# A narrower dense tile in a two-branch streaming layer: 192 tokens by gathered expert rows, projected ahead of the other 384

## The reference, cut to what matters

```python
x = x + (g_m * a_m + g_f * a_f + g_c * a_c) @ p['w_out']
x = x + peer_ffn(rmsnorm(x, p['norm_ffn']), wq, keys, u, v)

def peer_block(tok, wq, keys, u, v):
    qr = (tok @ wq).reshape(p, PEER_HEADS, 2, PEER_DQ // 2)
    s = jnp.einsum('phcd,hckd->phck', qr, keys)
    top_s, top_i = lax.top_k(s, PEER_TOPK)
    cand = top_s[:, :, 0, :, None] + top_s[:, :, 1, None, :]
    ids = top_i[:, :, 0, :, None] * N_KEYS + top_i[:, :, 1, None, :]
    best, j = lax.top_k(cand.reshape(p, PEER_HEADS, PEER_TOPK * PEER_TOPK), PEER_TOPK)
    eidx = jnp.take_along_axis(ids.reshape(...), j, axis=-1)
    g = jax.nn.softmax(best, axis=-1)
    act = jax.nn.gelu(jnp.einsum('phkd,pd->phk', u[eidx], tok))
    return jnp.einsum('phk,phkd->pd', g * act, v[eidx])
```

## Time and profile before

| | us |
|---|---|
| median of 3 runs (1950.44 to 1951.83) | 1951.48 |
| the profiled execution | 1951.0 |
| its span in the trace | 1949.3 |
| TensorE busy (97% of the span) | 1888.0 |
| VectorE busy (77%) | 1506.5 |
| GpSimd busy (48%) | 941.9 |
| ScalarE busy (44%) | 859.6 |

### The profile page before, as it was taken

How to read it: one execution, slowest core, us unless ns; L and a number is a source line. 1 busy time by engine, 2 the same in 40 slices (tenths; PEclk the granted TensorE clock), 3 DMA queues, 4 the chain that set the end, 5 groups by cost and what they waited for, 6 DMA issues and landing times.

```text
span 1949.3 us, 34536 instructions
## 1 busy us (share of the span) xinstructions
PE 1888.0 (97%) x12585; PEld 1215.4 (62%) x12596; DVE 1506.5 (77%) x2995; ACT 859.6 (44%) x1313; POOL 941.9 (48%) x586
## 2 busy tenths in 40 slices
PE   9999999999999999999999999998599999999997
PEld 7647777777777776555556666654255555555554
DVE  7975566454355568999899899846798999999885
ACT  6444446555443433333356666642233333333331
POOL 3732222222243353666877777878544445454320
PEclk9999999999999999999999999999799999999998
DMA  5722114223352223777989999999999999999971
GB/s 201 220 100 97 47 55 131 88 86 129 122 155 88 97 77 111 233 271 267 354 281 380 382 378 375 375 326 366 362 379 370 380 394 399 384 400 386 398 284 49
DMA packets 165532, 486.17 MB, mean 249 GB/s; under 512 B 17688, under 2 KB 59744, under 8 KB 164904
## 3 DMA queue, kind: packets, MB, share of 16 engines
q1 hardware_dynamic: 81824, 240.98, 34.4%
q0 software_dynamic: 46208, 167.83, 23.1%
q10 hardware_dynamic: 37384, 75.84, 10.5%
HBM read 419.75 MB, written 64.80 MB: 249 GB/s over the span
## 4 chain that ended last, share of the span: by engine, by line
PE 75%; DVE 14%; POOL 5%; issue 3%; DMA 1%; ACT 1%; ACTq 0%; DVEq 0%; POOLq 0%; SPq 0%
PE ps L2304 27%; PE ps L1847 24%; PE ps L1966 10%; PE ps L1863 3%; POOL w_lo L585 3%; POOL rows L618 3%; DVE rows L1635 2%; PE ps L2120 1%; PE ps L2244 1%; PE ps L2245 1%; DVE eq L1622 1%; DVE eq L1620 1%; PE ps L2100 1%; DVE eq L1619 1%; PE ps L2178 1%
## 5 line engine op out<-in xcount | busy, mean ns | idle before, releaser
L585 POOL TENSOR_TENSOR w_lo<-raw,w_hi 128x1024 bf16<-128x1024 f32 x229 | 503.1, 2201 | 609.6 <-ACT w_hi L695 586.1
L695 ACT ACTIVATE w_hi<-raw 128x1024 bf16<-128x1024 f32 x357 | 374.3, 1051 | 313.8 <-DMA raw<-in_v_units 129.1
L2304 PE MATMUL ps<-W_hi,w_hi 128*128 128x416 bf16 x992 | 337.5, 340 | 25.8 <-DVE W_lo L1771 25.8
L1847 PE MATMUL ps<-act_hi,w_hi 128*128 128x416 bf16 (+1 forms) x1040 | 351.6, 339 | 6.8 <-ACT hb L1055 6.0
L1847 PE MATMUL ps<-act_lo,w_hi 128*128 128x416 bf16 (+1 forms) x1040 | 351.6, 339 | 0.0
L1847 PE MATMUL ps<-act_hi,w_lo 128*128 128x416 bf16 (+1 forms) x1040 | 351.5, 339 | 0.0
L2304 PE MATMUL ps<-W_lo,w_hi 128*128 128x416 bf16 x992 | 337.4, 340 | 0.0
L2304 PE MATMUL ps<-W_hi,w_lo 128*128 128x416 bf16 x992 | 337.4, 340 | 0.0
L618 POOL DMA_INDIRECT rows<-in_v_units,rowi x128 | 170.4, 1331 | 202.1 <-DVE accS L1743 179.8
L1055 ACT ACTIVATE hb<-ps 128x416 f32<-128x416 f32 x128 | 66.2, 517 | 275.9 <-PE ps L1847 261.7
L1721 DVE TENSOR_TENSOR w_lo<-raw,w_hi 128x1024 bf16<-128x1024 f32 x124 | 151.2, 1219 | 43.0 <-ACT w_hi L695 42.9
(11 more groups left out here) (453 smaller groups left out, 3488.4 us busy)
## 6 DMA issues: line engine op xcount, KB each, us to landing
raw<-in_u_units SPq DMA_DIRECT2D x128, 512.0 KB, 5.5
raw<-in_v_units SPq DMA_DIRECT2D x128, 512.0 KB, 10.2
raw<-in_units SPq DMA_DIRECT2D x99, 512.0 KB, 3.3
hd<-hb ACTq DMA_DIRECT2D x128, 224.0 KB, 5.7
Hb<-hd SPq DMA_DIRECT2D x32, 896.0 KB, 8.4
gd<-gsb ACTq DMA_DIRECT2D x48, 448.0 KB, 7.0
Gb<-gd SPq DMA_DIRECT2D x32, 672.0 KB, 6.2
gz<-stage ACTq DMA_DIRECT2D x24, 288.0 KB, 2.1
```

The lines of the kernel that those rows point to most:

```text
L585: pool.tensor_tensor(w_lo[:, k % RING, :], raw[:, k % RAW, :], w_hi[:, k % RING, :], ALU.subtract).then_inc(lo_ready, 1)
L695: act.activation(w_hi[:, k % RING, :], raw[:, k % RAW, :], ACT.Copy).then_inc(hi_ready, 1)
L1847: last = pe.matmul(ps[:, bank + half, 0:n], w[:, slot, col:col + P], x(k)[:, half * n:(half + 1) * n], start=(k == 0 and w is w_hi and x i ...
L2304: ins = pe.matmul(ps[:, d, 0:TDX], w[:, slot, d * P:(d + 1) * P], x[:, k, 0:TDX], start=(first and w is w_hi and x is W_hi), stop=False)
```

## The change

- 192 tokens are gathered: the last 128 as before, and 64 more (`NX` = P/2) that lie two partitions to a token, 64 rows on each. They are now ordinary members of one list of `ND` = 192 dots and 192 sums: `x_dot`, the move across partitions and the separate table are gone. 384 tokens (`TD`) are dense, and everything stored is 384 wide; a block of routes has 48 tokens (`TBLK`), six steps a body, 48 steps in all (`G_BODY`, `N_STEP`).
- Output and query projection run twice, once for the 192 tokens (`NA`) and once for the 384; the 24 units are loaded and split a second time (`U_OUT2`, `U_WQ2`).
- VectorE makes the routes of the first tile between the additions of the second output projection (`out_beside`, `OUT_AT`), and 12 of the dots between the sortings of the second query projection (`DOTS_WQ`, `DOTS_AT`). GpSimd issues 18 fetches in that projection.
- The routing products begin one body sooner (`J_G` 5 for 6), with two dots a step (`DOTS_TWO` = 4, in a pair of steps, for 3); the remaining 44 dots follow, two a unit.
- In the second expert half GpSimd makes the low half of every fourth unit, from unit 7 on (`pool_makes`), VectorE the others. `x_combine` follows every second `combine`.
- SBUF is laid out anew.

```diff
-NX = 32
-TDX = TD - NX
+NX = P // 2
+ND = NST + NX
+T0 = T - NSP
+TD = T0 - NX
+NA = T - TD
...
-J_G = 6
+J_G = 5
...
-G_BODY = 7
+G_BODY = 6
...
+DOTS_WQ, DOTS_AT = 12, 4
...
-DOTS_TWO = 3
+DOTS_TWO = 4
+OUT_AT = (1, 2, 4, 6, 10, 15, 17, 18)
...
+def pool_makes(c):
+
+    return c >= 2 * GRP - 1 and c % GRP == GRP - 1
...
             for c in range(NCH):
                 fetch_v(n_main(c), v_rows, rowi[:, c:c + 1])
-                i = (c - X_COMB) // X_STEP
-                if c == X_COMB + X_STEP * i and 0 <= i < NX:
-                    fetch_v(n_comb(i), v_rows, rowx[:, i:i + 1])
+                if c + GRP < NCH and pool_makes(c + GRP):
+                    pool.wait_ge(hi_ready, U_V + c + GRP + 1)
+                    pool.tensor_tensor(w_lo[:, (U_V + c + GRP) % RING, :], raw[:, (U_V + c + GRP) % RAW, :],
+                                       w_hi[:, (U_V + c + GRP) % RING, :], ALU.subtract).then_inc(v_pool_low, 1)
+                if c % 2:
+                    fetch_v(n_comb(c // 2), v_rows, rowi[:, NST + c // 2:NST + c // 2 + 1])
...
+            for q in range(NHC):
+                dve.wait_ge(s_ready, NHC + q + 1)
+                top16(step1, lambda x: ps[:, 4 + q % 2, x * P:(x + 1) * P], lambda x: rest[:, x, :],
+                      lambda x: top[:, 1 + x, q, :], lambda x: topi[:, 1 + x, q, :], NFT - 1)
+                if 0 <= q - DOTS_AT < DOTS_WQ:
+                    dot(q - DOTS_AT)
...
-            for s in range(NX):
-                x_dot(s)
             dve.wait_ge(b_prod, N_STEP)
             for c in range(NCH + LAG):
                 if c < NCH:
                     gated(c)
-                if N_VLOW <= c + 2 < NCH:
+                if N_VLOW <= c + 2 < NCH and not pool_makes(c + 2):
                     unit_low(c + 2)
...
+            pe.wait_ge(r2_kept, 1)
+            for j in range(KT):
+                n = U_OUT2 + j
+                pe.wait_ge(lo_ready, n + 1)
+                if j == 2:
+                    pe.wait_ge(tk1, 4 * NHC)
+                if j >= 4:
+                    pe.wait_ge(x2_ready, KT + j - 3)
+                tile(n % RING, lambda k: mg_hi[:, k, mB], lambda k: mg_lo[:, k, mB], OUT_BANKS[j % 4], n=TD,
+                     halves=1).then_inc(unit_used, 1)
+                if j == TOK_AT:
+                    turn_tokens()
...
+            pe.wait_ge(x2_ready, 2 * KT)
+            pe.wait_ge(x_kept, 1)
```

More of the change, by code:

```diff
@@ new lines, in _, with turn_tokens @@
+                if q:
+                    key_scores_a(q - 1)
+            key_scores_a(NHC - 1)
+            def turn_tokens():
+                pe.wait_ge(h_scaled, KT)
+                pe.wait_ge(half_kept, NHC)
+                pe.wait_ge(q_evac, NHC)
+                for x in range(KT):
+                    last = pe.transpose(ps[:, 6 + x // 4, x % 4 * P:(x % 4 + 1) * P], hA[:, x, NX:NA], ident[:, :])
+                last.then_inc(tok_turned, 1)
+                for b in range(2):
+                    for x in range(KT):
+                        last = pe.matmul(ps[b * HP:(b + 1) * HP, 2 + x // 4, x % 4 * P:(x % 4 + 1) * P], hA[:, x, 0:NX],
+                                         ident[:, :], start=True, stop=True)
+                last.then_inc(x_turned, 1)
@@ new lines, in key_scores, with token_sums @@
+            def key_scores(q):
+                pe.wait_ge(q_evac, NHC + q + 1)
+                if q >= 2:
+                    pe.wait_ge(tk1, 4 * (NHC + q - 2) + 2)
+                for t in range(NFT - 1):
+                    last = pe.matmul(ps[:, 4 + q % 2, t * P:(t + 1) * P], qrB[:, q % 2, t * P:(t + 1) * P], keys[:, q, :],
+                                     start=True, stop=True)
+                last.then_inc(s_ready, 1)
+            def token_sums():
+                pe.wait_ge(n_add, (KT - 1) * 4)
+                for t in range(NFT - 1):
+                    last = pe.matmul(ps[:, 0, t:t + 1], sqB[:, 0, t * P:(t + 1) * P], ones[:, 0:1], start=True, stop=True)
+                last.then_inc(n_ssq, 1)
@@ new lines, in token_rows @@
+            def token_rows():
+                pe.wait_ge(n_inv, 4)
+                for t in range(NFT - 1):
+                    last = pe.matmul(ps[:, 1, t * P:(t + 1) * P], rB[:, 1, t:t + 1].broadcast_to((P, P)), ident[:, :], start=True,
+                                     stop=True)
+                last.then_inc(r2_spread, 1)
+            pe.wait_ge(x2_ready, 2 * KT)
+            pe.wait_ge(x_kept, 1)
+            for q in range(NHC):
+                n = U_WQ2 + q
+                pe.wait_ge(lo_ready, n + 1)
+                if q >= 2:
+                    pe.wait_ge(q_evac, NHC + q - 1)
+                tile(n % RING, lambda k: xg_hi[:, k, mB], lambda k: xg_lo[:, k, mB], 2 + q % 2, n=TD, halves=1,
+                     ready=None if q else 3 * KT).then_inc(unit_used, 1)
```

645 lines of the change are left out of this document (348 added, 297 removed).

## The result

The changed kernel takes **2085.97 us** (median of 4 runs, 2078.27 to 2095.8) against 1950.96 us for the kernel before on the same chip (4 runs, 1949.81 to 1951.83): ratio **1.0695**, 95% interval 1.0648 to 1.0742. I had predicted 1914 us, in a range of 1872 to 1950, with a chance of 0.12 for slower. The profiled execution took 2078.27 us, with a span of 2076.4 us and a mean granted clock of 0.969.

The account below looks back on a forecast made before the run. DMA was taken to bound the kernel from the routing products on: first routing product at 958 us, second half from 1369, its 512 and 10 us to 1891, tail 21 to 1912, forecast 1914 us; range 1872 to 1950.

Parts of the forecast that it names:

- What bounds it, and what the dense part saves: Whole kernel: DMA as full as TensorE; 384-column tiles save TensorE 82 us over 256 units, 112 us all together.
- The low halves given to GpSimd I cost at nothing, covered by DMA: Second expert half: GpSimd's low halves cost nothing under DMA's 4.18 us a unit; worth 16 us if DMA had room.
- four units' lead: Second expert half: GpSimd's low half stands behind a waiting fetch, but is made four units ahead.
- VectorE's durations in the first half: Stretch of routing products: DMA 300 us and 4 for a slack start, weighed against TensorE; no term for VectorE.
- My slower rival: From 958 us on: DMA falls under 376 GB/s as late units run the queues dry; 1966 us, chance 0.15.
- 103 us: Last 22 units before the second half: DMA moves 41.3 MB at 400 GB/s in 103 us, where TensorE needs 86.
- The part ahead of the experts: Both output and query passes: first expert product at about 773 us in place of 753.8, 19 us given away.
- Hidden, just: Passes of the 192 gathered tokens: GpSimd's 53 us of low halves fit within the 59 us these passes take.
- 396 GB/s: Second half: DMA moves 202.8 MB at 396 GB/s in 512 us, with 10 us more to the last product.
- the two slower rivals: DMA under 376 GB/s, 1966 us, chance 0.15; memory the limit, 346 GB/s at a full share, 2034 us, chance 0.02.
- the 1999 us for a lower bandwidth: The forecast's sum at the Trainium skill's 358 GB/s, one core's share of memory, would end at 1999 us.
- The stall of 25.8 us: TensorE's wait before the second half goes, since all 192 dots are now made in the first half.

Follow-up runs that it names:

- the first experiment: The changed kernel, but VectorE makes all low halves of the second expert half again and GpSimd none: 2049.3 us.
- the run with the least GpSimd work: Changed kernel with 64-column GpSimd low halves from second query pass through first expert half, fetches up to three units earlier, no GpSimd low halves in second half: 1915.85 us.

## Why the prediction was wrong

- **What bounds it, and what the dense part saves: the saving was there.** With GpSimd's subtractions next to gone the kernel ran in 1915.85 us, where I had 1914. The agreement is luck in part: the first routing product came 15 us earlier (943.0 for 958), the routing products were 16 us shorter, and the second half 31 us longer (556.7 for 525.5).
- **"The low halves given to GpSimd I cost at nothing, covered by DMA": the step that failed, in the second half.** They cost 24 us (21 to 25 over the runs). I compared GpSimd's load with the time it had (10.2 of 16 us) and never asked what its 2.20 us do to VectorE's 1.28. Some 14 us came from the order; the other 10 I put down to holding, by the durations. The "four units' lead" was no cover: it made the low half ask for a high half that wasn't there yet, with the next fetch behind it.
- **VectorE's durations in the first half: the step that failed there, and the largest.** I worked the routing stretch out for DMA and TensorE alone, 304 us, and not for VectorE. There 48 steps and 96 dots meet 64 low halves of GpSimd, and each of these costs the stretch 0.7 to 1.0 us (47 to 64 us over 64): with the fetches early VectorE was busy 347.65 of 349.1 us, and with the subtractions short the stretch took 290.9. The kernel before showed it to anyone who compared two groups of one shape. Between 1030 and 1260 us it had:

```profile
L1701 DVE TENSOR_TENSOR hot<-iota,pair 128x1024 bf16<-128x1024 bf16 x41 | 57.3, 1396 | 7.5 <-PE ps L2245 7.5
L1705 DVE TENSOR_TENSOR hot_lo<-hot,pair 128x1024 bf16<-128x1024 bf16 x41 | 28.1, 686 | 0.0
```

  Two operations of the same kind and size, 1396 and 686 ns. One by one, 28 of the 41 took 0.84 us or more, and all 28 lie over a subtraction of GpSimd; the others took at most 0.75. No run took the subtractions out of this kernel, but by what the changed kernel's runs show it was a hold already, paid where VectorE had 16 us of 230 to spare.
- **The fetches' place.** I did not price the order of GpSimd's list in this stretch: each fetch stands behind a low half that waits for ScalarE. That was 17 to 34 us. My slower rival had this chain (a late unit holds a combination, that a fetch, and the queues run dry), with a price of 52 us and a chance of 0.15; its place was the second half, where it proved to be about 14 us.
- **"103 us" for the last 22 units: 134.7.** I had them bound by DMA, and GpSimd bounds them: one low half of 2.2 us and two fetches a unit. With short subtractions the stretch took 110.
- **The part ahead of the experts: 773, measured 787.8.** The pass of the 192 tokens ended at 660.95 us, 14 us late for 647; the 45 us for the second output pass came out. A query unit of the first pass took 2.70 us for my 2.50, some 3 us over the 16, and the rest lies ahead of them, in the output units and the norm. "Hidden, just" weighed GpSimd there against TensorE and not against VectorE. Five of VectorE's eight low halves of the tokens (`xg_lo`, 0.40 us at their shortest) took some 2.0 us, each beside GpSimd's subtractions:

```profile
L1602 DVE SCALAR_TENSOR_TENSOR xg_lo<-xT,par,xg_hi x8: 401/2016/2150, 597.0 to 616.3; 128x192 bf16<-128x192 f32 x8
```

  No run shortened the subtractions of this first pass, so that holding made it late is read from the durations. The 7 us that a run did win are of the second pass, which I had not put too low.
- **"396 GB/s": 384 to 387, and slower at both ends.** 203.5 MB took 557.5 us, 365 GB/s over all. The mid stretch at 384 is 3% under what I took, 16 us; the rest of the 31 us are the ends. From 2000 to 2015 us the first experiment's kernel moved 198 GB/s.
- **A slip in the sums.** The times of the two slower rivals, 1966 and 2034, and the 1999 us for a lower bandwidth leave out the 4 us of slack that the forecast's own sum has: each would be 4 us more. Nothing hangs on it.
- **The stall of 25.8 us** is gone, as predicted. In its place 16.9 us of TensorE waiting for ScalarE's hb before the routes, which I had as "some 20".

## What to carry to other kernels

Before work is given to GpSimd, count it twice: its time there, and its time as idle time of VectorE, wherever VectorE works on two SBUF operands. A group whose mean is far over the mean of its twin of the same shape is held by something, and the gap is the price where that engine is full. In a list that an engine works in order, a transfer must not stand behind an operation that waits for another engine; here moving the transfers up to three units was worth some 20 us, and taking the subtraction off that list, which ends the holding too, 50 more.

## What the runs showed of the chip that I had not expected

- A VectorE instruction with two operands in SBUF can last its own time and GpSimd's whole subtraction besides (0.26 us became 2.80 beside 2.13), and GpSimd's is longer in turn where it meets VectorE's (3204 ns on average from 1600 to 1900 us, 2131 in the run with the low half two units ahead). With one operand in PSUM there is no such effect: 57 of the 60 dots of the kernel before from 1030 to 1260 us lie over a subtraction, and none took more than 1.22 us.
- Without that, DMA delivered more than I had dared to take: 405 GB/s from 940 to 1220 us in the run with the least GpSimd work, with results being written at the same time, over 280 us:

```profile
940.00:1220.00 280.00, 275.88 (x2155) 182.34 (x2154) 230.43 (x382) 168.87 (x164) 137.75 (x157) 0.99 1.02 405
```

- The second half, which only reads, gave less (384 to 387) at the same full share. Why the mix with 1.5 gathers a unit is slower was not tried.
